# Heads of the second block in pairs: turned outputs, GpSimd scaling ahead of the turn, one run of w_o units

## What is computed

```python
s = einsum('bqhd,bkhd->bhqk', q, k) * scale        # MLA; masked causally
p = softmax(where(mask, s, NEG_INF), -1)
o = einsum('bhqk,bkhd->bqhd', p, v)
# dilated: outs and log-sum-exps of three (window, dilation) pairs, joined by their softmax
o = concatenate([o_a, o_b, o_c], -1)               # 16 heads x 64 = 1024
mix = einsum('bsc,cd->bsd', o, w_o)
x = layer_norm(ALPHA * x + mix, ln1_g, ln1_b)      # then a mixture of experts, layer_norm
```

## Time and profile before

| | us |
|---|---|
| runs of the kernel before | 1723.4, 1724.02, 1725.14 (median 1724.02) |
| span of the profiled execution, first to last instruction | 1722.0 |
| difference of that span to the median | 2.0 |
| PE busy | 1698.4 (99%) |
| VectorE (DVE) busy | 867.6 (50%) |
| ScalarE (ACT) busy | 657.9 (38%) |
| GpSimd (POOL) busy | 135.1 (8%) |
| DMA moved | 396.65 MB |

### The profile page before, as it was taken

The page is one execution under the profiler, slowest core; times in us unless marked ns, Lnnn a source line. Parts: engine busy times, 40 slices in busy tenths (PEclk is TensorE's granted clock), DMA queues, the critical chain, the costliest instruction groups (busy, mean ns, idle before and its releaser), DMA issues. The chain is left out here.

```text
span 1722.0 us, 24194 instructions
## 1 busy us (share of the span) xinstructions
PE 1698.4 (99%) x9811; PEld 1303.5 (76%) x9811; DVE 867.6 (50%) x1412; ACT 657.9 (38%) x928; POOL 135.1 (8%) x194
## 2 busy tenths in 40 slices
PE   9999999999999999999999999999999999999997
PEld 7888889999888888999898885555449888555553
DVE  6566564444647566444468655322236864532223
ACT  5456444333544544333344632112124453222111
POOL 1020001111102000111111000000001100000000
PEclk9999999999999999999999999999999999999999
DMA  8544545553644454555366238999975613899994
GB/s 310 186 137 144 186 155 186 182 193 115 235 164 147 159 183 147 196 181 185 106 235 187 74 114 339 421 420 422 421 289 199 183 67 129 351 421 421 421 421 182
DMA packets 151677, 396.65 MB, mean 230 GB/s; under 512 B 19984, under 2 KB 84496, under 8 KB 126992
## 3 DMA queue, kind: packets, MB, share of 16 engines
q1 hardware_dynamic: 151568, 395.18, 61.6%
HBM read 394.10 MB, written 1.05 MB: 229 GB/s over the span
## 5 line engine op out<-in xcount | busy, mean ns | idle before, releaser
L825 PE MATMUL ps<-split,split 128*128 128x256 f32 (+3 forms) x1872 | 631.1, 337 | 1.0 <-DVE split L818 0.7
L829 PE MATMUL ps<-split,split 128*128 128x256 f32 (+3 forms) x1872 | 627.6, 335 | 0.1
L826 PE MATMUL ps<-split,split 128*128 128x256 f32 (+3 forms) x1872 | 623.6, 333 | 0.0
L803 DVE TENSOR_TENSOR split<-ring,split 128x2048 fp32r<-128x2048 f32 x136 | 312.4, 2303 | 255.1 <-ACT split L796 255.1
L829 PEld LDWEIGHTS ps<-split,split 128*128 128x128 f32 x1872 | 351.9, 188 | 35.5 <-DVE split L2128 0.7
L825 PEld LDWEIGHTS ps<-split,split 128*128 128x128 f32 x1872 | 351.7, 188 | 35.5 <-issue 2.0
L826 PEld LDWEIGHTS ps<-split,split 128*128 128x128 f32 x1872 | 353.1, 189 | 33.5 <-issue 0.5
L796 ACT ACTIVATE split<-ring 128x2048 fp32r<-128x2048 f32 x136 | 260.3, 1915 | 279.0 <-PE ps L829 269.0
L2736 DVE SCALAR_TENSOR_TENSOR arena<-arena,ps 128x256 f32<-128x256 f32 x32 | 15.4, 481 | 167.9 <-ACT arena L2054 132.4
L818 DVE TENSOR_TENSOR split<-ring,split 128x1536 fp32r<-128x1536 f32 (+3 forms) x44 | 80.7, 1850 | 29.1 <-ACT split L812 28.9
L812 ACT ACTIVATE split<-ring 128x1536 fp32r<-128x1536 f32 (+3 forms) x44 | 67.7, 1546 | 69.9 <-PE ps L829 64.8
(11 more groups left out here) (265 smaller groups left out, 2005.2 us busy)
## 6 DMA issues: line engine op xcount, KB each, us to landing
ring<-in_w_in SPq DMA_DIRECT2D x52, 1024.0 KB, 4.9
ring<-in_w_gate_up SPq DMA_DIRECT2D x44, 1024.0 KB, 5.2
ring<-in_expert_w_gate SPq DMA_DIRECT2D x32, 1024.0 KB, 10.6
ring<-in_expert_w_up SPq DMA_DIRECT2D x32, 1024.0 KB, 12.7
ring<-in_expert_w_down SPq DMA_DIRECT2D x32, 1024.0 KB, 12.3
ring<-in_w_down SPq DMA_DIRECT2D x22, 1024.0 KB, 4.8
ring<-in_w_in SPq DMA_DIRECT2D x28, 768.0 KB, 4.4
high<-in_expert_w_gate SPq DMA_DIRECT2D x16, 1024.0 KB, 9.5
```

What stands on the lines that cost most here:

```text
L803: nc.vector.tensor_tensor(split(slot), slot, split(high[:, n % HIGH, :]), ALU.subtract).then_inc(low_done.sem, 1)
L825: nc.tensor.matmul(acc, sh, mh, start=start, stop=False)
L826: nc.tensor.matmul(acc, *second, start=False, stop=False)
L829: return nc.tensor.matmul(acc, *third, start=False, stop=stop)
```

## The change

- `JOB_PAIRS` takes the jobs in pairs, the dilated ones first: (12, 13), (14, 15), (8, 9), (10, 11), then the MLA heads. `pair_scores` issues the matmuls of the two heads in turns, into two banks. Two DSA or dilated heads hold rows 0 to 63 and rows 64 to 127 of PE.
- `pair_out` makes the values stationary (64 columns) and lets the turned weights move (256 and 128 columns). The output is turned already: head h of a pair lies on partitions 64h to 64h + 63 of one bank. The "oT" transposes, `mix` and the copy to `xn` go; `high_out` and `low_out` split each pair's bank straight into T8.
- So the softmax is scaled before the turn. VectorE takes a reciprocal per head (`invert`), then GpSimd multiplies the head's exps in place by it (two `tensor_scalar`, 128 x 128 and 128 x 256, dilated 128 x 384 and 128 x 768), and only then does PE turn them (`normed`).
- The turned blocks leave PSUM in parts of 384 columns, half by ScalarE and half by VectorE.
- The first pair's scores go ahead of the second half of projection `v1`. Three warming matmuls (`keep_running`) ahead of the first scores go.
- On ScalarE high part 18 goes behind the dqT copies, 19 between the exps of pairs 0 and 1, 20 behind the last exps; VectorE's low parts follow them.
- The w_o units are taken in the order 3, 2, 0, 1 and all stand behind the last pair.

```diff
@@ PE
-                project2("v1", l)
...
+                project2("v1", l, units_=(0,))
+                pe.wait_ge(dqT_in.sem, dqT_in.at(l, 3))
+                pe.wait_ge(dkT_in.sem, dkT_in.at(l, 3))
+                pair_scores(0, l)
+                project2("v1", l, units_=(1,))
+                pair_scores(1, l)
+                pe.wait_ge(dsT_in.sem, dsT_in.at(l, 1))
+                pair_scores(2, l)
+                pair_turn(0, l)
+                pair_scores(3, l)
+                pair_turn(1, l)
...
+                pair_out(0, l)
...
+                for p in range(4, 8):
+                    pair_scores(p, l)
+                    pair_turn(p - 2, l)
+                    pair_out(p - 3, l)
+                pair_turn(6, l)
+                pair_out(5, l)
+                pair_turn(7, l)
+                pair_out(6, l)
+                pair_out(7, l)
+                for n in range(4):
+                    output_unit(n, l)
@@ pair_out
+                    for kt_ in range(2):
+                        for h, j in enumerate(JOB_PAIRS[p]):
+                            E = e_of(p, h, c)
+                            o = acc[h * HD:(h + 1) * HD, :]
...
+                                mm = nc.tensor.matmul(o[:, 0:SEQ], values(j, c, 0), E[:, 0:SEQ], start=(c == 0),
+                                                      stop=False)
...
+                                mm = nc.tensor.matmul(o[:, P:SEQ], values(j, c, 1), E[:, SEQ:TRI], start=False,
+                                                      stop=last)
@@ ScalarE
+                weigh(0)
                 high_parts2(19, 19, l)
                 chunk("v1")
...
+                weigh(1)
+                for p in range(2, 8):
+                    weigh(p)
+                    turned(p - 2)
+                    if p >= 4:
+                        high_out(p - 4)
+                high_out(4)
+                high_parts2(20, 20, l)
+                turned(6)
+                high_out(5)
+                turned(7)
+                high_out(6)
+                high_out(7)
@@ VectorE
+                mask(0, 0)
+                mask(0, 1)
+                invert(0, 0)
+                low_parts2(19, 19)
+                invert(0, 1)
+                mask(1, 0)
+                mask(1, 1)
+                invert(1, 0)
+                dve.wait_ge(nm_masked.sem, nm_masked.at(l, 1))
+                for p in range(2, 8):
+                    mask(p, 0)
+                    invert(p - 1, 1)
+                    mask(p, 1)
+                    turned(p - 2)
+                    invert(p, 0)
+                    if p >= 4:
+                        low_out(p - 4)
+                invert(7, 1)
+                low_out(4)
+                low_parts2(20, 20)
+                turned(6)
+                low_out(5)
+                turned(7)
+                low_out(6)
+                low_out(7)
@@ GpSimd
+                for p, pair in enumerate(JOB_PAIRS):
+                    for h, j in enumerate(pair):
+                        wait_apart(pool, recip.sem, recip.at(l, 2 * p + h + 1))
...
+                            last = nc.gpsimd.tensor_scalar(S[:, lo:hi], S[:, lo:hi], rinv[:, j, t:t + 1], None,
+                                                           ALU.mult)
+                        last.then_inc(normed.sem, 1)
```

More of the change, by code:

```diff
@@ L199, in parts, with part_counts @@
 def parts(j):
-    return 0 if not 0 <= j < JOBS else 3 if j >= HM + HX else 1
+    return 3 if j >= HM + HX else 1
+def part_counts():
+    masked_at, turned_at = {}, {}
+    by_engine = [0, 0]
+    for pair in JOB_PAIRS:
+        for h, j in enumerate(pair):
+            for part in range(parts(j)):
+                masked_at[j, part] = len(masked_at) + 1
+                engine = (h + part) % 2
+                by_engine[engine] += 1
+                turned_at[j, part] = (engine, by_engine[engine])
+    return masked_at, turned_at, by_engine
 def duo_units(pass_, d):
@@ L683, in build @@
         for kp in range(4):
[L684 to L685 removed]
+            read2["xT", kp] = (bT_low, kp + 5)
             read2["xT2", kp] = ((xT2_act, xT2_dve)[kp % 2], 2 * (kp // 2) + 2)
@@ L1436, in head_scores @@
                     return
                 for part, which in enumerate(((0, 1), (2,))):
-                    acc = claim2(("S", j, part), l)
+                    accs = [claim2(("S", j, part), l) for j in pair]
                     for n, c in enumerate(which):
-                        q, k = ops[c]
-                        mm = nc.tensor.matmul(acc[:, n * SEQ:(n + 1) * SEQ], q[:, P:SEQ], k, start=True, stop=True)
-                    fill(mm, ("S", j, part))
-                acc = claim2(("S", j, 2), l)
@@ new lines, in pair_scores @@
+                        for h in range(2):
+                            q, k = ops[h][c]
+                            mm = nc.tensor.matmul(accs[h][:, n * SEQ:(n + 1) * SEQ], q[:, P:SEQ], k, start=True,
+                                                  stop=True)
+                            if c == which[-1]:
+                                fill(mm, ("S", pair[h], part))
+                accs = [claim2(("S", j, 2), l) for j in pair]
+                for c in range(3):
+                    for h in range(2):
+                        q, k = ops[h][c]
+                        mm = nc.tensor.matmul(accs[h][:, c * P:(c + 1) * P], q[:, 0:P], k[:, 0:P], start=True, stop=True)
+                        if c == 2:
+                            fill(mm, ("S", pair[h], 2))
@@ new lines, in pair_turn @@
+            def pair_turn(p, l):
+                for h, j in enumerate(JOB_PAIRS[p]):
+                    pe.wait_ge(normed.sem, normed.at(l, 2 * p + h + 1))
+                    for part in range(parts(j)):
+                        acc = claim2(("E", j, part), l)
+                        blocks = (0, 1, 2) if parts(j) == 1 else (6 + part, 2 * part, 2 * part + 1)
+                        for i, blk in enumerate(blocks):
+                            mm = nc.tensor.transpose(acc[:, i * P:(i + 1) * P],
+                                                     s_of(p, h)[:, blk * P:(blk + 1) * P], ident[:])
+                        fill(mm, ("E", j, part))
@@ new lines, in output_unit @@
+            def output_unit(n, l, js=(0, 1)):
+                u = WO_ORDER[n]
+                w = weights2(("w_o_2", u), l)
+                by_j = [(j, i) for j in js for i in range(4)]
+                by_bank = [(j, i) for i in range(4) for j in js]
+                for j, i in by_bank if n == 3 else by_j:
+                    t, half = divmod(i, 2)
+                    last = n == 3 and j == 1
+                    if n == 0 and j == 0:
+                        claim2(("wo", i), l)
+                    low = None
+                    if i == 0:
+                        pe.wait_ge(bT_high.sem, bT_high.at(l, KT + 2 * n + j + 1))
+                        low = bT_low.sem, bT_low.at(l, KT + 2 * n + j + 1)
+                    mm = product3(bank2(("wo", i)), X(2 * u + j, slice(t * P, (t + 1) * P)),
+                                  [a[:, j, half * 512:(half + 1) * 512] for a in w],
+                                  start=(n == 0 and j == 0), stop=last, low=low)
+                    if last:
+                        fill(mm, ("wo", i))
+                if n < 3 and js[-1] == 1:
+                    mm.then_inc(unit_read2.sem, 1)
@@ new lines, in turned, with high_out @@
+                def turned(p):
+                    for h, j in enumerate(JOB_PAIRS[p]):
+                        for part in range(parts(j)):
+                            if turned_at[j, part][0] == 0:
+                                leave2(("E", j, part), l, e_of(p, h, part), ET_act, width=TRI)
+                def high_out(p):
+                    nc.scalar.activation(split(T8[:, JOB_PAIRS[p][0] // 2, :]), content2(("O", p), l)[:, 0:SEQ],
+                                         ACT.Copy).then_inc(bT_high.sem, 1)
@@ new lines, in invert, with turned @@
+                def invert(p, h):
+                    j = JOB_PAIRS[p][h]
+                    dve.wait_ge(weighed.sem, weighed.at(l, 2 * p + h + 1))
+                    nc.vector.reciprocal(rinv[:, j, :], lsum[:, j, :]).then_inc(recip.sem, 1)
+                def turned(p):
+                    for h, j in enumerate(JOB_PAIRS[p]):
+                        for part in range(parts(j)):
+                            if turned_at[j, part][0] == 1:
+                                leave2(("E", j, part), l, e_of(p, h, part), ET_dve, width=TRI)
```

323 lines of the change are left out of this document (134 added, 189 removed).

## The result

| | before | changed |
|---|---|---|
| median of 9 runs each | 1723.84 us | 1727.43 us |
| lowest and highest | 1721.96, 1726.53 | 1725.64, 1729.02 |
| ratio to before | | 1.0021, 95% interval 1.0012 to 1.0031 |
| span of the profiled execution | 1722.0 us | 1724.2 us |

The change makes the kernel slower by 3.6 us, where I had forecast 6.8 us faster; the time lies above my range. The profiled execution of the changed kernel is the fastest of its nine.

A forecast was written before the change was run, and what follows sets the result against it. Queue order on the other engines, not PE's 28 us, was to bound the heads. Per layer 5.0 saved, less 0.4 and 1.2 for clock, gives 3.4; 6.8 for both takes 1724.0 to 1717.2 us, range 1709 to 1723.

The forecast's parts named there:

- the chain: Hand-worked sequence of waits through layer 0's heads: w_o starts at 998.5 in place of 1003.49, 5.0 us saved.
- POOL's price: GpSimd's new multiply: 1.5 ns a column, 15 us per layer; upper end 27 by the two-input row.
- the clock: Low clock some 3 us behind each of two long PE idles: costs 0.4 us first, 1.2 in the tail, per layer.
- PE's work: Heads stage, per layer: scores, turns and outputs on PE take 28 us in place of 45.85.
- If PE stayed the bound: Heads stage: with PE still the limit, w_o would start some 17 us earlier; forecast not to happen.
- Step 1: Before pair 2's scores: pair 1's masks queue behind VectorE's low part 19, so PE idles 4.8 us.
- Steps 2 and 3: Pair 0's turn and pair 3's scores wait, PE idles 1.1 us more; then PE is nearly fed until 989.5.
- Step 4: Tail: last turns and outputs wait behind high and low part 20; PE idles 4.3 us, w_o starts at 998.5.
- That rival: GpSimd at its upper price: pair 1 scaled 1.5 us late, tail 0.5; 2 us less per layer, 1721; chance 0.12.
- Evacuation alone: Heads: emptying PSUM bounds, not the waits; w_o near 990, 13 us per layer, 1698, or half, 1706; chance 0.07.
- The held clock: Clock stays up through both gaps of the heads stage: 10 us saved in all, 1714.0; chance 0.20.
- No packing: Paired heads' matmuls don't overlap: 13 us more per layer, idles hiding some 8; 1727; chance 0.07.

The follow-up runs named there:

- e13: Changed kernel with VectorE's list padded, first gap and both tail gaps warmed, GpSimd's multiplies left out, splits in their old places: 1720.38 us.
- e5: Changed kernel with splits 19 and 20 moved behind the last pair's outputs on ScalarE and VectorE, and VectorE's list padded: 1712.47 us.
- e9: Changed kernel with VectorE's list padded and warming matmuls (8 and 6) in the two tail gaps: 1720.63 us.
- e15: Changed kernel with VectorE's list padded, tail gaps warmed, GpSimd's multiplies left out, first gap not warmed: 1718.56 us.
- e2: Changed kernel without GpSimd's multiplies, so the division by the softmax sums is left out of the second block: 1725.33 us.
- e4: Changed kernel with 65 more instructions in a never-run branch of VectorE's list: 1725.11 us.
- e14: Changed kernel with VectorE's list padded, first gap and both tail gaps warmed, GpSimd's scaling kept: 1721.78 us.
- e6: Changed kernel with splits 19 and 20 behind the last outputs, VectorE's list padded, GpSimd's scaling left out: 1706.32 us.
- e8: Changed kernel with late splits 19 and 20, VectorE's list padded, and each pair's second head scaled on VectorE instead of GpSimd: 1709.32 us.
- e1: Changed kernel with splits 19 and 20 moved behind the last pair's outputs on ScalarE and VectorE, list not padded: 1713.64 us.
- e3: Changed kernel with 18 warming matmuls in the first gap, before the scores of pair 2: 1727.62 us.
- e10: Changed kernel with late splits 19 and 20, padded list, and each pair's two heads issued one after the other: 1710.16 us.
- e12: Changed kernel with late splits, padded list, scaling shared by GpSimd and VectorE, and 7 warming matmuls in the first gap: 1709.38 us.

## Why the prediction was wrong

**What failed, in short.** I forecast w_o 5.0 us earlier in each layer, 3.4 with the clock; the stages got 0.44 and 0.10 us shorter. The bound moved to the waits, as forecast, and at the places forecast, but steps 2 to 4 of the chain handed over too fast (3.0 us over both layers, by e13), POOL's price was too low (2.1 us), the clock was set too cheap (1 us or so), and 2.2 us at the end of VectorE's list weren't in the sum.

**PE's work: right.** Pairs at 0.65 us, MLA pairs at 1.4, a dilated pair's scores in 954.36 - 952.19 = 2.17 us for the 2.16 forecast, which was one head's before:

```profile
952.19 1.57 PE L1480 MATMUL ps<-arena 64*128 64x256 f32 x12
953.59 0.83 PE L1488 MATMUL ps<-arena 64*128 64x128 f32 x12
954.36 0.44 PE L863 MATMUL ps<-split,split 128*128 128x384 f32 x1
```

"If PE stayed the bound" w_o would have been 17 us earlier; it didn't stay.

**Step 1, the masks behind low part 19: right in size** (4.85 for 4.8), but taking 19 away gave 0.9 us in the medians, 4.9 in the profiled stages of both layers, and not twice 4.8: what it held back was waiting for GpSimd next (e5).

**Steps 2 and 3: 2 us late.** PE came to pair 0's scores 1.2 us ahead of my clock (952.19 for 953.4), but to output 0 at 975.16, where my sum had its end at 976.5 and so its start, three groups of 0.65 earlier, at 974.55. Counted from pair 0's scores, that is 23.0 us in place of 21.1. e13, with clock and GpSimd out of the way, has 21.6, so these two, set too low, made most of it.

**Step 4, the tail: the right mechanism, and the most costly of all; its handoffs failed.** I forecast 4.3 us of idle and 1.2 for the clock, 11.0 us for both layers; taking split 20 away gave 11.7. That the two agree so well is in part luck: the clock makes more of it than I gave it (4.5 us in both layers by e9, for 2.4), the idles less. And the step's handoffs were short: in e13 the last turn starts 44.7 us behind pair 0's scores (43.7 in my chain) and needs 2.1 us to w_o, not 1.4.

**POOL's price: a term that failed.** I took 1.5 ns a column from the nearest row with one tensor input; the multiply with a scalar read from memory costs 2.5 ns a column and 0.3 us fixed, above even the upper end I drew from the two-input row. That rival had 0.12 and 1721, 3.8 us above my forecast. By e15 against e9 and e2 against the changed kernel the whole scaling is worth 2.1 us here, so its price alone doesn't explain the miss.

**The clock: mis-sized.** 6 us or more at the lower level, in three places of four, for the 3 taken from the router. The first gap's 0.4 was nothing, the tail's 1.2 was 2.2.

**Not in the sum at all: the end of VectorE's list**, 2.2 us of the span and 2.3 of the median (e4).

In the profiled execution I was off by 1724.2 - 1715.2 = 9.0 us. Both layers together: the list makes 2.2. The stages took 137.8 us where my chain gives 69.27 + 69.04 - 10.0 = 128.3, and w_o 0.6 more than before; less the 3.2 that I had set for the clock, 6.9 are left. Of these GpSimd makes 1.7 to 3.4 (stages of e9 to e15, e14 to e13; 2.2 by e2), the clock 0.7 to 1.3 net, and handoffs that I set too short the rest, some 3; e13 has 1.7 of them in layer 0 and 46.4 - 45.1 = 1.3 in layer 1. That the sum closes is in part luck: the changed kernel reached mqT 1.3 us earlier than the kernel before, and lost 1.2 outside the stages and w_o, and I have no cause for either. The median lies 3.2 us above the profiled span, where I took 2.0, so the sum there was off by 9.0 + 1.2 = 10.2.

**The rivals.** Evacuation alone (1698, or 1706) is near what e6 measured, 1706.3, once splits and scaling were out of the way, and PE's waits in its layer 0, 5.1 us in the heads, are all for copies and masks of ScalarE and VectorE. But PE is busy there for 32.72 of 38.00 us (956 to 994), so evacuation takes its part without being shown to bound, and e6 is another kernel than the one forecast. The Trainium skill ("TensorEngine Tiling (Array Packing)", section "PSUM Bottleneck") says that the copy out of PSUM may become the bottleneck. e6's waits fit this; in the change as made the waits were mostly for the splits. The held clock (1714.0) is refuted as a forecast by the clock rows and as arithmetic by e13. No packing is refuted by the 0.65 us, although its number, 1727, is the one measured: a time alone doesn't tell the cause. None of my rivals was slower by several small terms of one sign, which is what happened.

**My chances.** 0.75 for faster rested on a margin of 6.8 us, from which in the end every open term (price, clock, handoffs, list) took away. Of the two that I had bounded, the handoffs came near their end (1.7 and 1.3 us of my 2 a layer), and POOL's price came out above its.

## What to carry to other kernels

When an edit takes work off the engine that bounds, the queues of its helpers decide what is kept: look for wide instructions (here splits of 1.9 and 2.3 us) that stand ahead of short ones on which the engine waits, above all in the last rounds, and move them behind the last such handoff before judging the edit. The change as made cost 3.6 us; the same change with four queue entries moved gained 10.4, and with the new work shared with the cheaper engine and the list padded 14.5. An idle is worth what comes next behind it: 19's gap of 4.85 us a layer was worth 0.9 us in all by the medians and 4.9 by the profiled stages, 20's two gaps of 3.4 us a layer 11.7 and 8.0, because little else was waiting there and the clock fell with them.

## What was unexpected of the hardware

- **GpSimd's multiply by a per-row scalar**: 607, 928, 1248 and 2207 ns for 128, 256, 384 and 768 columns, against 298, 347, 736 and 609 ns on VectorE for the same forms in e8 (the last two from two instructions each).
- **The end of an instruction list has a place.** Four kernels with this list (changed, e1, e2, e3) have VectorE's last instruction 2.1 us behind the others; eleven with 65 more unused ones don't. The Trainium skill ("Runtime: NRT & Kernel Launch", section "Instruction fetch mechanics") says that lists are fetched in blocks ahead of execution, that crossing a block is mostly hidden, and that a taken branch out of the window forces a fetch. VectorE's list ends behind a branch it jumps over; a fetch in the open would fit. No row shows it directly, and only two lengths of the list were tried.
- **Two heads in different halves overlap whatever the order** of their matmuls (e10: 0.70 us from one pair's output group to the next, either way), up to two of one head in a row.
- **The router's stretch varies by itself.** Between its first matmul and the ranks, with the same code, lie 6.9, 7.9 or 9.4 us, by how long the low clock lasts there. The 12 warming matmuls ahead of the ranks, in e5 and in e1:

```profile
1026.66 2.76 PE L1112 MATMUL ps<-ones 128*128 128x512 bf16 x12
```

```profile
1027.39 5.31 PE L1112 MATMUL ps<-ones 128*128 128x512 bf16 x12
```

In the kernel before the same place has 7.9 and 6.9. It may well make much of the spread between runs of one kernel, but only one execution of each is profiled, so that isn't shown. Whether a fully fed heads stage makes the longer forms more frequent (e9 has 7.9 and 9.5, e12 9.5 and 7.9, but e5 and e13 6.9 twice) stays open too. It would explain why e13 gains 1.4 us a layer on e9 in its stages and next to nothing in the median.
